# Feed-forward values turned in 32x32 blocks by VectorE instead of 128x128 on TensorE, in a two-layer hybrid block

## The reference

```python
# layer 1
h2 = rms_norm(x, g_ffn)
gate, up = jnp.split(h2 @ w_ffn_in, 2, axis=-1)
return x + (jax.nn.silu(gate) * up) @ w_ffn_out
# layer 2
h = rms_norm_2(x, ffn_norm_w[l])
x = x + (jax.nn.silu(h @ ffn_w_gate[l]) * (h @ ffn_w_up[l])) @ ffn_w_down[l]
```

## Time and profile before

| what | value |
|---|---|
| median of three timed runs | 2826.79 us |
| profiled execution, own time | 2826.68 us |
| its span | 2824.8 us |
| TensorE busy | 2799.2 us, 99% |
| VectorE busy | 1606.6 us, 57% |
| ScalarE busy | 1205.1 us, 43% |
| chain that ended last, TensorE's share | 94% |
| HBM read | 497.13 MB, 177 GB/s over the span |

### The profile page before, as it was taken

How to read it: one execution, slowest core, us unless ns; L and a number is a source line. 1 busy time by engine, 2 the same in 40 slices (tenths; PEclk the granted TensorE clock), 3 DMA queues, 4 the chain that set the end, 5 groups by cost and what they waited for, 6 DMA issues and landing times.

```text
span 2824.8 us, 38637 instructions
## 1 busy us (share of the span) xinstructions
PE 2799.2 (99%) x16570; PEld 2366.6 (84%) x16570; DVE 1606.6 (57%) x1374; ACT 1205.1 (43%) x1070; POOL 84.4 (3%) x138
## 2 busy tenths in 40 slices
PE   8999999999999999999999999999999999999998
PEld 7888888888888888888888888998888888888887
DVE  6768554454555454544446688977564544544445
ACT  4464443333443343433335455544343333333333
POOL 0100000000000000002001100030000000000000
PEclk9999999999999999999999999999999999999999
DMA  7555555555555555555555655400455555555554
GB/s 240 173 171 187 164 170 190 191 194 194 183 189 191 187 186 193 188 184 193 194 194 196 204 166 179 150 3 33 149 181 192 192 185 187 192 193 182 193 194 176
DMA packets 258173, 501.57 MB, mean 178 GB/s; under 512 B 12870, under 2 KB 18321, under 8 KB 257665
## 3 DMA queue, kind: packets, MB, share of 16 engines
q1 hardware_dynamic: 257905, 499.33, 54.0%
q10 hardware_dynamic: 144, 0.39, 0.0%
HBM read 497.13 MB, written 2.10 MB: 177 GB/s over the span
## 4 chain that ended last, share of the span: by engine, by line
PE 94%; DVE 3%; ACT 1%; SPq 1%; issue 0%; DMA 0%; ACTq 0%; DVEq 0%
PE psum L790 24%; PE psum L791 24%; PE psum L792 24%; PE psum L760 9%; PE psum L759 5%; PE psum L1248 2%; DVE weight_lo L2085 1%; PE psum L841 1%; ACT weight_hi L1561 1%; PE psum L740 1%; PE psum L743 1%; PE psum L742 1%; PE psum L694 0%; SPq L482 0%; DMA weight_raw<-in_w_in 0%
## 5 line engine op out<-in xcount | busy, mean ns | idle before, releaser
L2085 DVE TENSOR_TENSOR weight_lo<-weight_raw,weight_hi 128x2048 fp32r<-128x2048 f32 x459 | 1052.3, 2293 | 1048.8 <-ACT weight_hi L1561 1047.0
L1561 ACT ACTIVATE weight_hi<-weight_raw 128x2048 fp32r<-128x2048 f32 x459 | 879.6, 1916 | 1374.5 <-PE psum L792 1199.6
L790 PE MATMUL psum<-weight_hi,h_both 128*128 128x512 f32 x1856 | 725.1, 391 | 0.9 <-DVE weight_lo L2085 0.9
L792 PE MATMUL psum<-weight_hi,h_both 128*128 128x512 f32 x1856 | 722.5, 389 | 0.0
L791 PE MATMUL psum<-weight_lo,h_both 128*128 128x512 f32 x1856 | 722.1, 389 | 0.0
L760 PE MATMUL psum<-h_both,weight_hi 128*128 128x512 f32 x1264 | 442.4, 394 | 0.0
L792 PEld LDWEIGHTS psum<-weight_hi,h_both 128*128 128x128 f32 x1856 | 348.4, 188 | 72.9
L790 PEld LDWEIGHTS psum<-weight_hi,h_both 128*128 128x128 f32 x1856 | 348.5, 188 | 72.6 <-DVE weight_lo L2085 1.4
L791 PEld LDWEIGHTS psum<-weight_lo,h_both 128*128 128x128 f32 x1856 | 348.6, 188 | 71.3
L759 PE MATMUL psum<-h_both,weight_lo 128*128 128x256 f32 x1264 | 356.8, 282 | 5.6 <-DVE proj L2160 3.2
L760 PEld LDWEIGHTS psum<-h_both,weight_hi 128*128 128x128 f32 x1264 | 236.8, 187 | 53.5
(11 more groups left out here) (545 smaller groups left out, 2238.7 us busy)
## 6 DMA issues: line engine op xcount, KB each, us to landing
weight_raw<-in_w_in SPq DMA_DIRECT2D x143, 1024.0 KB, 5.3
weight_raw<-in_w_ffn_in SPq DMA_DIRECT2D x88, 1024.0 KB, 5.0
weight_raw<-in_w_ffn_out SPq DMA_DIRECT2D x44, 1024.0 KB, 5.0
weight_raw<-in_ffn_w_gate SPq DMA_DIRECT2D x44, 1024.0 KB, 5.1
weight_raw<-in_ffn_w_up SPq DMA_DIRECT2D x44, 1024.0 KB, 5.2
weight_raw<-in_ffn_w_down SPq DMA_DIRECT2D x40, 1024.0 KB, 5.0
weight_raw<-in_w_out SPq DMA_DIRECT2D x32, 1024.0 KB, 5.0
weight_raw<-in_w_branch_rnn SPq DMA_DIRECT2D x8, 1024.0 KB, 4.9
```

What stands on the lines that cost most here:

```text
L790: mm(acc[:, t, :], xh[:, c], wh[:, k, :], start=(start and k == 0), stop=False, skip_group_check=True)
L792: last = mm(acc[:, t, :], xl[:, c], wh[:, k, :], start=False, stop=(stop and k == CK - 1), skip_group_check=True)
L1561: A(hi[j % g.hi][:], raw[j % g.ring][:], ACT.Copy).then_inc(hi_ready, 1)
L2085: V.tensor_tensor(lo[r][:], raw[r][:], hi[j % g.hi][:].bitcast(F32), ALU.subtract).then_inc(lo_ready, 1)
```

## The change

The eight transposes of `turn_ffn` are gone. VectorE turns `act_up` itself, with block transposes: one instruction takes 32 partitions and writes each 32x32 block of them turned. For each group `a` of 32 tokens (input partitions) there are four instructions, one for each group `c` of 32 columns within every 128 (output partitions), with 2 x 4 x 32 = 256 elements per partition. The result `Ft` is an SBUF tile of 4 KB per partition that lies where the last body's part of `Fl` will be. Rounding and subtraction read `Ft` instead of PSUM. The four groups are spread over chunks 1 to 4 of the next body; ScalarE's rounding moves from after chunk 3 to after chunk 6, VectorE's subtraction from after chunk 3 to after chunk 7. At the end of each feed-forward input the four groups stand among the first three chunks of the output product, and ScalarE rounds after chunk 2 rather than chunk 1. TensorE waits for the eleventh split before chunk 0 of output body 1 rather than chunk 2 of body 0.

```diff
--- before.py
+++ after.py
@@ -138,6 +138,7 @@
         gated_sum = at("gated_sum", [P, 2, CN], TO + 24 * KB)
         Fh = at("ffn_hi", [P, FT, T], HO, F32R)
         Fl = at("ffn_lo", [P, FT, T], HO + FT * KB, F32R)
+        Ft = at("ffn_turned", [P, CK, T], HO + FT * KB + (FT - CK) * KB)
         act_gate = at("ffn_act", [P, 2, CN], HO + 2 * FT * KB)
         act_up = at("ffn_act_up", [P, 2, CN], HO + 2 * FT * KB + 4 * KB)
 
@@ -833,14 +834,6 @@
                         if c == 1 and s % 6 == 0 and (i or s):
                             turn_merged(2 * i + s // 6 - 1)
 
-            def turn_ffn(n_parts):
-
-                pe.wait_ge(ffn_up, n_parts)
-                for k in range(4):
-                    for t in range(2):
-                        last = tr(pair(2)[:, k, t * P:(t + 1) * P], act_up[:, t, k * P:(k + 1) * P], ident[:])
-                last.then_inc(ffn_turned, 1)
-
             def up_body(g, i, n, n_norm=0, last_turn=None):
 
                 first = isinstance(i, int) and i == 0
@@ -855,8 +848,6 @@
                         product_tokens(g, i, 4 * s + c, token_pair(s), lambda k: h_rhs(CK * c + k), c == 0, c == 3)
                         if first and s == 0 and c == 0 and last_turn:
                             last_turn()
-                        if not first and s == 0 and c == 1:
-                            turn_ffn(n * g.bodies + i)
 
             def ups(g, n, n_norm, last_turn=None):
                 up_body(g, 0, n, n_norm, last_turn)
@@ -920,11 +911,9 @@
                     for j in range(4):
                         if i == 0 and j == 0:
                             pe.wait_ge(strips_out, g.sbase)
-                        if i == 0 and j == 2:
+                        if i == 1 and j == 0:
                             pe.wait_ge(ffn_split, n * (FF // CN))
                         product_tokens(g, i, j, token_pair(j), lhs(i), i == 0, i == g.bodies - 1)
-                        if i == 0 and j == 0:
-                            turn_ffn(n * (FF // CN))
                         if n_norm and i == g.bodies - 1 and j > 0:
                             pe.wait_ge(x_ready, j)
                             turn_x(j - 1, j - 1, X)
@@ -1747,15 +1736,15 @@
 
             def ffn_high(g, n, i):
                 act.wait_ge(ffn_turned, n * g.bodies + i + 1)
-                A(Fh[:, bass.ds(4 * i, 4), :], pair(2), ACT.Copy).then_inc(ffn_hi, 1)
+                A(Fh[:, bass.ds(4 * i, 4), :], Ft[:], ACT.Copy).then_inc(ffn_hi, 1)
 
             def up_split(g, n, i, j0=0):
                 for j in range(j0, g.per):
                     chunks(g, i, j, j + 1)
-                    if j == 3 and not (isinstance(i, int) and i == 0):
-                        ffn_high(g, n, i - 1)
                     if j == 5:
                         ffn_sigmoid(g, n, i)
+                    if j == 6 and not (isinstance(i, int) and i == 0):
+                        ffn_high(g, n, i - 1)
 
             def out_ffn(wo, up, dn, n_norm, n, rhs):
 
@@ -1774,9 +1763,9 @@
                 up_split(up, n, 0, 4)
                 with act.Fori(1, up.bodies) as i:
                     up_split(up, n, i)
-                chunks(dn, 0, 0, 2)
+                chunks(dn, 0, 0, 3)
                 ffn_high(up, n, up.bodies - 1)
-                chunks(dn, 0, 2, 4)
+                chunks(dn, 0, 3, 4)
                 with act.Fori(1, dn.bodies - 1) as i:
                     chunks(dn, i, 0, 4)
 
@@ -2432,22 +2421,32 @@
                                                           ALU.mult, ALU.mult)
                         last.then_inc(ffn_up, 1)
 
+                def turned(i, a):
+                    dve.wait_ge(ffn_up, n * g.bodies + i + 1)
+                    for c in range(4):
+                        last = V.transpose(Ft[32 * c:32 * c + 32].rearrange("p k (t q m) -> p t k q m", t=2, q=4)[:, :, :, a, :],
+                                           act_up[32 * a:32 * a + 32].rearrange("p t (k c j) -> p t k c j", k=4, c=4)[:, :, :, c, :])
+                    if a == 3:
+                        last.then_inc(ffn_turned, 1)
+
                 def finished(i):
                     dve.wait_ge(ffn_hi, n * g.bodies + i + 1)
                     fh, fl = Fh[:, bass.ds(4 * i, 4), :], Fl[:, bass.ds(4 * i, 4), :]
-                    V.tensor_tensor(fl, pair(2), fh.bitcast(F32), ALU.subtract).then_inc(ffn_split, 1)
-                return taken, finished
-
-            def up_split(g, i, taken, finished, j0=0):
+                    V.tensor_tensor(fl, Ft[:], fh.bitcast(F32), ALU.subtract).then_inc(ffn_split, 1)
+                return taken, turned, finished
+
+            def up_split(g, i, taken, turned, finished, j0=0):
                 first = isinstance(i, int) and i == 0
                 for j in range(j0, g.per):
                     chunks(g, i, j, j + 1)
                     if j == 1 and not first:
                         taken(i - 1, 1)
-                    if j == 3 and not first:
-                        finished(i - 1)
+                    if 1 <= j < 5 and not first:
+                        turned(i - 1, j - 1)
                     if j == 5:
                         taken(i, 0)
+                    if j == 7 and not first:
+                        finished(i - 1)
 
             def out_ffn(wo, up, dn, n_norm, gain, eps, n, j0):
 
@@ -2466,16 +2465,21 @@
                 low(*last)
                 chunks(up, 0, 3, 4)
                 inverse_root({1: 2, 3: 5}[n_norm], {1: 8, 3: 20}[n_norm], eps, ready=col_ready)
-                taken, finished = ffn(up, n)
-                up_split(up, 0, taken, finished, 4)
+                taken, turned, finished = ffn(up, n)
+                up_split(up, 0, taken, turned, finished, 4)
                 with dve.Fori(1, up.bodies) as i:
-                    up_split(up, i, taken, finished)
+                    up_split(up, i, taken, turned, finished)
                 last = up.bodies - 1
                 chunks(dn, 0, 0, 1)
                 taken(last, 1)
+                turned(last, 0)
                 chunks(dn, 0, 1, 2)
+                turned(last, 1)
+                turned(last, 2)
+                chunks(dn, 0, 2, 3)
+                turned(last, 3)
                 finished(last)
-                chunks(dn, 0, 2, 4)
+                chunks(dn, 0, 3, 4)
                 with dve.Fori(1, dn.bodies - 1) as i:
                     chunks(dn, i, 0, 4)
```

## The result

The changed kernel took 2811.87 us (median of 5 runs, 2809.56 to 2813.94), the one before 2826.34 beside it: ratio 0.9950, 95% interval 0.9938 to 0.9961. The profiled execution took 2812.94 us (span 2811.2), 13.7 less than the 2826.68 of before. Forecast were 2811 and a gain of 15.9 us.

What follows compares the result with a forecast made beforehand. The prediction took TensorE's chain of matmuls (99% busy) to bound the kernel: 2826.7 us, less 20.2 for removed transposes, plus 4.3 for stalls at the ends, gives 2810.8, said as 2811; range 2806 to 2820.

Steps and rivals of the forecast that it cites:

- What goes, 20.2 us: TensorE's transposes in 22 feed-forward bodies leave the path, 0.92 us a set, 20.2 us in all.
- The transposes' duration, s = 0.43: One VectorE transpose of 32 partitions, 256 elements each, takes s = 0.43 us, bounds 0.28 and 0.69.
- No overlap: VectorE's four transposes of a set write different partition groups and do not overlap: 4 x 0.43 = 1.72 us.
- Nothing in the loop: In the feed-forward input loop VectorE's transposes fit idle slots after chunks 1 to 4 and cost 0.
- The tight slot: Loop chunk 1 on VectorE: transposes end at 992.95, the next subtraction starts at 993.01, so they fit.
- the slack: In the loop, VectorE's subtraction of a weight chunk ends 0.9 us before TensorE needs that chunk.
- 4.3 us at the ends: First three output chunks after each feed-forward input: stalls of 0.3, 0.3 and 1.5 us, 4.3 for two feed-forwards.
- The rule for 128x128 transposes: Skill rule sending these to TensorE where PSUM will do; by it the change would lose, by the rows only the ends.
- The sum: Whole kernel: 2826.7 - 20.2 + 4.3 = 2810.8, said as 2811 us.
- the slow rival: VectorE's set overflows its slots at chunks 1 to 4 of 20 bodies; slower than before from s = 0.79; chance 0.06.
- the prediction's own condition for chunk 1: In the loop, stalls appear at chunk 1 when 4s is over 2.67, that is s over 0.67.
- What to look for in the waits: L790's waits for L2085 grow from 0.9 to about 5 us, six more stalls at the first three output chunks.

Runs made afterwards that it cites:

- the last two experiments: Against the changed kernel: every set of transposes in the input loop made twice, 2861.61 us; sixteen transposes in two slots of eight, 2810.57 us.
- both reorderings: Against the changed kernel: end sets spread one per output chunk, 2805.23 us; at the ends only rounding and subtraction of the values moved one chunk later, 2806.95 us.
- the doubled kernel: Changed kernel with every set of four transposes in the input loop made twice, the second into another tile: 2861.61 us, ratio 1.0130.
- the two timed comparisons: Changed kernel against the kernel before, timed twice: 2811.87 against 2826.34 us, and repeated unchanged, 2809.80 against 2825.56 us.
- `same_groups`: Changed kernel with each transpose writing the partition group it reads, so the output is another: 2808.33 us, ratio 0.9944 against the kernel before.

## Why the prediction was right, step by step

- **What goes, 20.2 us.** 0.92 a set was forecast; the stretches give 0.91 in the loop and 1.06 at the ends, 20.3 us. Right.
- **The transposes' duration, s = 0.43.** It is 0.436. The 128x512 transpose row and the 32x256 row together were enough, though neither has this shape: strides and crossed partition groups together cost at most 0.03 over the 0.411 of the 32x256 operation.
- **No overlap.** Steps are 0.45 (1.78 for four), and 0.34 where a set stays within one output group. The two L2827 operations had shown it. The Trainium skill ("VectorE: DVE Perf Modes", the section on two Vector instructions with no wait between them) states that an instruction is held until all earlier ones are done when its output starts in another quadrant than the last one; the traces agree, with 0.45 against 0.34 from start to start.
- **Nothing in the loop.** Right to 0.01 us a loop, shown by leaving the transposes out. The tight slot was full where 0.06 was to be left over; this did not matter because of the slack, whose size the last two experiments bear out.
- **4.3 us at the ends.** They cost 5.2 (2.6 each), so this term was undersized by a fifth. The mechanism is shown by both reorderings: 1.6 of each 2.6 are ScalarE's rounding of a weight queued behind its wait for the last set, 1.0 is VectorE's backlog in the first two chunks. Forecast were stalls of 0.3, 0.3 and 1.5; TensorE is late by 0.35, 0.47 and 1.64. Most of that difference is the step of 0.447 in place of 0.43, 0.27 for sixteen of them. The other 0.14 had no term in the sum: the first chunk behind the last stall takes 5.58 rather than 5.44. It stands behind the stalls of the doubled kernel too, with 0.15. Why matmuls start further apart behind a stall, no run here shows.
- **The rule for 128x128 transposes.** The Trainium skill's section "Rules for kernel authors" prefers TensorE for them. VectorE did spend 7.0 us a body (16 x 0.436) where TensorE spent 0.92, and the kernel still became faster, because VectorE's idle time lay in the right slots. With twice that work a body (14 us) the kernel is slower than with TensorE's transposes.
- **The sum.** 2826.7 - 20.3 + 5.2 = 2811.6 by the stretches; the two timed comparisons gave gains of 14.5 and 15.8. The time came out at the forecast's 2811 with some luck, since chance between executions moves it by a few us, more than the 0.9 by which the ends were undersized.
- **The break-even of the slow rival** was put too high. It adds up the whole stretch from chunk 1 to chunk 5 and finds s = 0.79. By the prediction's own condition for chunk 1 (a stall of 4s - 2.67) the first slot alone stalls more than that up to s = 0.81, and 20 x (4s - 2.67) + 2 x (16s - 4.8) reaches 20.2 at s = 0.74. No run came near either.
- **What to look for in the waits** was put too simply. Forecast: L790's waits grow from 0.9 to about 5 us. The view shows 4.2 for L791, 3.2 of them at the ends, because it counts idle time behind matmul ends that are modelled; the stretches give 5.2 for the ends.

## What to carry to other kernels

An engine at 57% has room for other work only in its slots: add up, from its place in one period, the idle time ahead of each deadline and the slack that carries over, and set the new work into the slots one by one. Look separately at the places where the period is broken (the last iteration, the first of the next stage): here the loop lost nothing and the two ends lost 5.2 of 20.3 us, which one slot per set gave back. The dearest place for late work was a wait with the feed of the next stage queued behind it, 1.6 of each 2.6 us.

## Of the hardware

**Transposes that start behind another one.** In `same_groups` the second to fourth transpose of a set start about 0.07 us before the one ahead is over and last 0.39 to 0.40 us. The first of each set, which has nothing running ahead of it, lasts 0.43 to 0.44, although it reads and writes one group. In the changed kernel no transpose overlaps the one ahead, each lasts 0.432 to 0.442, and one that reads and writes the same group (the second of the second set: 0.434, started 0.45 behind the first) is no different from its neighbours. So crossing from one group to another costs nothing that shows. What costs is that the output group changes between two instructions, which takes the overlap away.

**The clock in layer 2's mixers.** No kernel here edits this stretch. It took 585.7 and 586.7 us in two executions and 587.8 to 588.7 in the other nine. In the two the granted clock stayed at its upper level (2.4 GHz) throughout the stretch; in the nine it fell to the lower (1.2 GHz) once, for a few us, at the 64x64 matmuls of the gated delta rule. Windows of before and of the changed kernel's second execution at that place (us, then busy us and instructions of PE, PEld, DVE, ACT and POOL, then granted clock, DMA share, GB/s):

```profile
1970.00:1976.00 6.00, 5.66 (x158) 5.38 (x155) 5.80 (x13) 1.60 (x2) 3.22 (x2) 1.00 0.02 5
1976.00:1984.00 8.00, 8.00 (x59) 7.88 (x58) 7.52 (x7) 4.09 (x6) 0.00 (x0) 0.57 0.52 179
```

```profile
1963.00:1969.00 6.00, 5.66 (x159) 5.38 (x156) 5.80 (x13) 1.61 (x2) 3.35 (x2) 1.00 0.03 7
1969.00:1977.00 8.00, 7.41 (x80) 7.30 (x81) 7.94 (x7) 5.08 (x7) 0.00 (x0) 1.00 0.63 214
```

Ahead of the fall TensorE did the same in both: 158 and 159 matmuls, busy 5.66 us of 6. Of two executions of the changed kernel one had the fall and one had not, so whether it comes is chance. The stretch is 1 to 3 us longer with it, where the change is worth 15. The page's tenths do not show it, so the prediction's upper level in every slice is true of the tenths and not of every us.
